# Two value phases of an expert layer: TensorE sums 512 columns of each row in place of 1024, VectorE 1536 in place of 1024

## The chip, the cores and the metric

The kernel runs on one core of a Trainium2 chip. The metric is the time of one execution on the device, in microseconds (us), lower is better. The engines have their own queues of instructions and meet only through semaphores: TensorE (PE in the rows: matrix products, with PEld for its weight loads), VectorE (DVE), ScalarE (ACT), GpSimd (POOL) and SyncE (SP). POOL and SP also start the transfers, which 16 DMA engines carry out.

## The reference

Two decoder layers are run over 256 prompt tokens and 32 sample tokens, each with 2048 features: a state-space mixer in layer 0, a gated recurrence in layer 1, and after each of them a mixer of experts. Each token picks 8 x 16 = 128 experts out of 16384. The part that matters here:

```python
def peer_ffn(h, w_q, sub_keys, u_emb, v_emb):
    idx, g = peer_retrieve(hf, w_q, sub_keys)        # top-16 of keys, top-16 of pairs, softmax
    ...
        u = u_emb[ib].astype(jnp.float32)
        act = jnp.einsum("nd,nhkd->nhk", xb.astype(jnp.float32), u)
        wgt = jax.nn.gelu(act, approximate=False) * gb
        v = v_emb[ib].astype(jnp.float32)
        return jnp.einsum("nhk,nhkd->nd", wgt, v)
```

So for each token 128 rows of the table u are fetched for dot products (a dot phase), and then 128 rows of the table v, which are weighted and summed (a value phase).

## The kernel before

Tokens lie on partitions: tiles 0 and 1 hold the 256 prompt tokens, tile 2 the 32 sample tokens four times over, so that it needs only 32 fetches per phase. One fetch, called a row below, is one gather of POOL (line 496): for each of 128 tokens the 2048 floats of its n-th expert, 1 MiB in all. It lands in one of 8 slots of a ring (`RING = 8`). All rows of all phases pass through this ring in order. POOL reuses a slot when VectorE is done with the row in it (`row_used`) and, in a value phase, TensorE too (`row_pe`); then it issues the next gather, for a row 8 further on.

A phase is named by layer and tile. Value phases come in the order of `PHASES`: (0, 0), (0, 2), (0, 1), (1, 0), (1, 2), (1, 1), with dot phases between them. In a value phase the sum of the weighted rows stays in PSUM in the four banks 4 to 7 (`high_banks`, 2048 columns). VectorE adds weight times row to the first columns (`v_row`, one SCALAR_TENSOR_TENSOR at line 1645 for each row). TensorE does the last columns: ScalarE scales the identity by the row's weights (`diagonals`, line 1259), and TensorE multiplies that diagonal matrix with the row, one matmul for each bank of 512 columns (line 923). A matmul of 32-bit floats stands as two records in the trace, so two banks are four records of a row. At the end VectorE adds TensorE's columns to the token tile (`last_columns`).

Other work is woven into the phases by row numbers (`Turns`: a step with number r is run after row r). Beside (0, 1) and (1, 0) run the queries and the choice of experts of the next layer or tile:

- TensorE multiplies the tokens with 16 slabs of weights (line 821), the first after row 16 of the phase and each next one 3 rows on, the last after row 61. A slab is 1 MiB that SP loads into a ring of 4 (`WRING`) when the product that used the slot is done. Behind every four products it makes key scores (lines 865 and 867).
- VectorE chooses the experts from the scores: top-16 lists of the keys, top-16 lists of the sums, and the expert numbers. Such a choice has three parts, and two rows stand between one part and the next. With the rows of the dot phase ahead taken off, `CHOOSE_ROW` puts the choices of (0, 1) after rows 30, 42, 54, 66 and 74, those of (1, 0) after rows 36, 48, 60 and 72. A softmax comes after row 84, and two norms come early in (0, 1).

Every row of VectorE waits for its gather and for VectorE's row before it:

```python
dve.wait_ge(row_in[r], 16 * (R + 1))
if n > 0:
    dve.wait_ge(row_used[(n - 1) % RING], ROUNDS * layer + V_AT[t] + (n - 1) // RING + 1)
```

Of the kernel before, what the change touches and what calls it, by code (L numbers as in the profile page):

```python
# [15 lines left out]
ALU = mybir.AluOpType  # L16
# [4 lines left out]
D = 2048  # L21
# [8 lines left out]
BANK = 512  # L30
# [22 lines left out]
PICKS_OF = [PICKS, PICKS, PICKS // COPIES]  # L53
# [7 lines left out]
LAST_HEAD_ISSUE = 6  # L61
LEAD = 3
GELU_SPLIT = 96
SHARE = 2
OWN = D - SHARE * BANK
DIAGS = 3
PHASES = [(0, 0), (0, 2), (0, 1), (1, 0), (1, 2), (1, 1)]

# [24 lines left out]
def values_before(layer, t):  # L93

    return sum(PICKS_OF[u] for _, u in PHASES[:PHASES.index((layer, t))])
# [59 lines left out]
def hybrid_step(nc, x, norms, slabs, keys, chan, s5_vec, s5_bc, s5_h0, lru_in, u0, v0, u1, v1,  # L155
                y_out, ys_out, s5p_out, s5s_out, lru_out):
    experts_u, experts_v = [u0, u1], [v0, v1]
    with ExitStack() as ctx:
        def sb(name, shape, dt=F32):
            return ctx.enter_context(nc.sbuf_tensor(name, shape, dt))  # L160

        def sem(name):
            return ctx.enter_context(nc.semaphore(name))


        X = sb("X", [P, TILES, D])
# [13 lines left out]
        ps = ctx.enter_context(nc.psum_tensor("ps", [P, 8, BANK], F32))  # L180
        hn_flat = HN[:].rearrange("p a b -> p (a b)")
        low_banks = ps[:, 0:4, :].rearrange("p b n -> p (b n)")
        high_banks = ps[:, 4:8, :].rearrange("p b n -> p (b n)")
        ht_flat = HT[:].rearrange("p a b -> p (a b)")

        def view(at, n, base=None):
            return (arena if base is None else base)[:, at:at + n]
# [58 lines left out]
        DG = [view(at - 512 + P * n, P) for n in range(DIAGS)]  # L246
# [23 lines left out]
        ring = view(0, RING * D).rearrange("p (r d) -> p r d", r=RING)  # L270
        ACC = HN[:, 2, :]
# [34 lines left out]
        row_used = [sem(f"row_used{r}") for r in range(RING)]  # L306
        row_pe = [sem(f"row_pe{r}") for r in range(RING)]
        diag_set, gate_set, v_done = sem("diag_set"), sem("gate_set"), sem("v_done")
# [314 lines left out]
        def _(pe):  # L623
# [289 lines left out]
            def value_rows(layer, t, turns):  # L913

                first = values_before(layer, t)
                if first > 0:
                    pe.wait_ge(v_done, PHASES.index((layer, t)))
                for n in range(PICKS_OF[t]):
                    R, r = ROUNDS * layer + V_AT[t] + n // RING, n % RING
                    pe.wait_ge(diag_set, first + n + 1)  # L920
                    pe.wait_ge(row_in[r], 16 * (R + 1))
                    for b in range(SHARE):
                        mm = nc.tensor.matmul(ps[:, 8 - SHARE + b, :], DG[(first + n) % DIAGS],  # L923
                                              ring[:, r, OWN + BANK * b:OWN + BANK * (b + 1)], start=(n == 0),
                                              stop=(n == PICKS_OF[t] - 1))
                    mm.then_inc(row_pe[r], 1)
                    turns.row()

            value_rows(0, 0, Turns(()))
            turns = Turns(sample_turn())  # L930
            value_rows(0, 2, turns)
            turns.finish()
            pe.wait_ge(norm_ht, 28)
            sample_sum(0)
            turned(7, 2)
            chain(0)
            turns = Turns(chain_queries(0))
            value_rows(0, 1, turns)
            turns.finish()
            turned(10, 1)  # L940
# [408 lines left out]
        def _(dve):  # L1349
            V = nc.vector  # L1350
# [151 lines left out]
            with dve.Fori(0, 4) as g:  # L1502
                for r in range(GROUP):
                    dve.wait_ge(bank_read, g * GROUP + (r + 3))
                    n = g * GROUP + r
# [126 lines left out]
            def v_row(layer, t, n):  # L1632

                R, r = ROUNDS * layer + V_AT[t] + n // RING, n % RING
                weight = WG[:, COL_AT[t] + n:COL_AT[t] + n + 1]
                dve.wait_ge(row_in[r], 16 * (R + 1))
                if n > 0:
                    dve.wait_ge(row_used[(n - 1) % RING], ROUNDS * layer + V_AT[t] + (n - 1) // RING + 1)
                row = ring[:, r, 0:OWN]
                if n == 0 and t == 2:  # L1640
                    V.tensor_scalar(high_banks[:, 0:OWN], row, weight, None, ALU.mult).then_inc(row_used[r], 1)
                    return
                total = X[:, t, 0:OWN] if n == 0 else high_banks[:, 0:OWN]
                to = high_banks[:, 0:OWN] if n < PICKS_OF[t] - 1 else ACC[:, 0:OWN] if t == 2 else X[:, t, 0:OWN]
                V.scalar_tensor_tensor(to, row, weight, total, ALU.mult, ALU.add).then_inc(row_used[r], 1)  # L1645

            def last_columns(layer, t):

                dve.wait_ge(row_pe[RING - 1], (values_before(layer, t) + PICKS_OF[t]) // RING + 1)
                if t == 2:  # L1650
                    V.tensor_copy(ACC[:, OWN:D], high_banks[:, OWN:D]).then_inc(v_done, 1)
                else:
                    V.tensor_tensor(X[:, t, OWN:D], high_banks[:, OWN:D], X[:, t, OWN:D], ALU.add).then_inc(v_done, 1)

            def u_rows(layer, t, turns, hn_count):

# [13 lines left out]
            def v_rows(layer, t, turns):  # L1670

                for n in range(PICKS_OF[t]):
                    if n == 0:
                        gate_weights(t, 0, GELU_SPLIT if t == 1 else PICKS_OF[t], 4 * layer + (1, 3, 2)[t])
                    if n == GELU_SPLIT and t == 1:
                        gate_weights(t, GELU_SPLIT, PICKS, 4 * layer + 4)
                    v_row(layer, t, n)
                    turns.row()
                last_columns(layer, t)
# [341 lines left out]
```

## Time and profile before

| | |
|---|---|
| median of 3 runs | 3864.35 us (3862.33 to 3864.55) |
| profiled execution, its own time and its span | 3864.24 us, 3862.4 us |
| PE busy (share of the span) | 2273.5 us (59%) |
| DVE busy | 2793.4 us (72%) |
| ACT busy | 679.6 us (18%) |
| POOL busy | 1472.3 us (38%) |
| DMA | 1404.76 MB, mean 364 GB/s |
| line 923, TensorE's columns of the rows | 1112.4 us in 2304 records |
| line 1645, VectorE's columns of the rows | 726.9 us in 564 instructions |

The busy times are sums over the whole span, in which engines work beside each other. The share of busy time is an average over stages with different limits; the value phase (0, 1) lies at 1900 to 2262 us of the span, (1, 0) at 2789 to 3139 us.

### The profile page before, as it was taken

The page shows a single profiled execution, that of the slowest core. Times are in us where ns is not written, and L with a number is a line of the kernel's source. Part 1 is how long each engine was busy: PE and PEld are TensorE (multiplying, and loading weights), DVE is VectorE, ACT ScalarE, POOL GpSimd, SP SyncE. Part 2 cuts the span into 40 slices and gives each one's busy share as a digit, 9 for nine tenths or more (in the row PEclk, how much of TensorE's full clock was granted, in tenths as well). Part 3 has the DMA queues.
Part 4 walks back from the last instruction along what each step waited for, and adds up shares of the span by engine and source line. Part 5 has one row for each costly group of instructions (what it writes and reads, how often), then busy time and mean ns, then how long its engine had stood idle before and what let it go on. Part 6 is the DMA issues. An engine that isn't in the chain of part 4 may idle for free.

```text
span 3862.4 us, 30909 instructions
## 1 busy us (share of the span) xinstructions
PE 2273.5 (59%) x9698; PEld 1381.5 (36%) x9698; DVE 2793.4 (72%) x3586; ACT 679.6 (18%) x1477; POOL 1472.3 (38%) x1739
## 2 busy tenths in 40 slices
PE   4667996000087788559599776470199773003776
PEld 2334775000022227549365246470055221001222
DVE  7996047999955558897757677868848658997554
ACT  6662121000011122120111112200011111000111
POOL 4885005434333343222323442223433434433432
PEclk8888998555599999779799998695599997556999
DMA  1002336999999999999999999999999999999998
GB/s 76 16 13 86 133 125 245 379 422 396 427 427 427 427 427 425 426 417 426 427 427 426 390 427 426 426 426 427 427 427 417 411 427 427 427 428 427 427 427 356
DMA packets 197426, 1404.76 MB, mean 364 GB/s; under 512 B 21952, under 2 KB 26304, under 8 KB 26768
## 3 DMA queue, kind: packets, MB, share of 16 engines
q0 software_dynamic: 167008, 1215.18, 74.9%
q1 hardware_dynamic: 30000, 187.74, 12.0%
q8 instruction: 73, 1.20, 0.1%
q14 instruction: 57, 0.47, 0.0%
q10 hardware_dynamic: 288, 0.18, 0.0%
HBM read 1399.77 MB, written 3.24 MB: 363 GB/s over the span
## 4 chain that ended last, share of the span: by engine, by line
DMA 38%; DVE 27%; PE 26%; issue 5%; ACT 4%; POOL 0%; POOLq 0%; DVEq 0%; ACTq 0%
DMA arena<-in_u_dram,ixs 26%; PE ps L923 16%; DVE arena L1629 12%; DMA arena<-in_v_dram,ixs 12%; PE ps L648 3%; ACT arena L1259 3%; PE ps L688 2%; DVE arena L1473 2%; PE ps L821 2%; DVE ps L1645 1%; DVE HN L1480 1%; DVE HN L1481 1%; DVE HN L1482 1%; DVE arena L1469 1%; DVE arena L1468 1%
## 5 line engine op out<-in xcount | busy, mean ns | idle before, releaser
L923 PE MATMUL ps<-arena 128*128 128x512 f32 x2304 | 1112.4, 612 | 1185.0 <-ACT arena L1259 1139.2
L1629 DVE CUSTOM_DVE_ANT_0 arena<-arena,ps 128x2048 f32<-128x2048 f32 x556 | 1257.4, 2286 | 193.4 <-DMA arena<-in_u_dram,ixs 175.0
L1645 DVE SCALAR_TENSOR_TENSOR ps<-arena,ps 128x1024 f32<-128x1024 f32 x564 | 726.9, 1289 | 588.1 <-DMA arena<-in_v_dram,ixs 576.0
L923 PEld LDWEIGHTS ps<-arena 128*128 128x128 f32 x2304 | 402.4, 191 | 1867.0 <-ACT arena L1259 938.6
L496 POOL DMA_INDIRECT arena<-in_u_dram,ixs x560 | 546.0, 975 | 1069.7 <-DVE arena L1629 1000.2
L496 POOL DMA_INDIRECT arena<-in_v_dram,ixs x576 | 556.3, 966 | 928.1 <-PE ps L923 719.5
L821 PE MATMUL ps<-HT,W 128*128 128x160 f32 (+1 forms) x3072 | 407.8, 295 | 70.6 <-ACT HN L1207 30.2
L821 PEld LDWEIGHTS ps<-HT,W 128*128 128x128 f32 x3072 | 402.4, 198 | 89.7 <-issue 74.5
L1259 ACT ACTIVATE arena<-ident,arena 128x128 f32<-128x128 f32 x576 | 228.2, 400 | 1003.0 <-PE ps L923 970.4
L849 PE MATMUL ps<-W,arena 128*128 128x128 f32 x1024 | 125.4, 283 | 41.0 <-DVE arena L1751 14.9
L849 PEld LDWEIGHTS ps<-W,arena 128*128 128x128 f32 x1024 | 121.7, 199 | 43.5 <-DVE arena L1751 15.1
L688 PE MATMUL ps<-HT,W 128*128 128x288 f32 x512 | 127.4, 410 | 0.0
L648 PE MATMUL ps<-arena,W 128*128 128x288 f32 x512 | 124.4, 406 | 0.7 <-ACT arena L1040 0.7
L833 PE MATMUL ps<-HN,W 128*128 128x160 f32 (+1 forms) x256 | 53.8, 381 | 98.6 <-ACT HN L1219 96.6
L1172 ACT ACTIVATE arena<-arena 128x32 f32<-128x32 f32 (+2 forms) x8 | 2.0, 260 | 623.6 <-DVE arena L1629 623.6
L688 PEld LDWEIGHTS ps<-HT,W 128*128 128x128 f32 x512 | 98.1, 193 | 27.8 <-issue 1.0
L648 PEld LDWEIGHTS ps<-arena,W 128*128 128x128 f32 x512 | 97.2, 190 | 27.5 <-issue 0.8
L754 PE MATMUL ps<-HN,arena 128*32 128x256 f32 x512 | 101.1, 481 | 0.0
L1506 DVE TENSOR_TENSOR arena<-arena 128x288 f32 x16 | 7.3, 458 | 127.2 <-ACT arena L1107 127.2
L1473 DVE TENSOR_TENSOR_SCAN arena<-arena 128x256 f32<-128x256 f32 x128 | 85.5, 736 | 0.5
L833 PEld LDWEIGHTS ps<-HN,W 128*128 128x128 f32 x256 | 48.9, 267 | 102.7 <-ACT HN L1219 98.9
L748 PE MATMUL ps<-HT,arena 128*128 128x256 f32 x32 | 18.8, 688 | 99.6 <-DVE HN L1482 99.6
(252 smaller groups left out, 2157.5 us busy)
## 6 DMA issues: line engine op xcount, KB each, us to landing
W<-in_slabs_dram SPq DMA_DIRECT2D x168, 1024.0 KB, 10.2
arena<-in_u_dram,ixs POOLq DMA_INDIRECT x576, 16.5
arena<-in_v_dram,ixs POOLq DMA_INDIRECT x576, 16.7
GB<-in_norms_dram POOLq DMA_DIRECT2D x4, 1024.0 KB, 6.2
arena<-in_s_bc_dram SPq DMA_DIRECT2D x32, 128.0 KB, 2.1
X<-in_x_dram SPq DMA_DIRECT2D x3, 1024.0 KB, 10.9
out_y_dram<-HN SPq DMA_DIRECT2D x2, 1024.0 KB, 6.3
arena<-in_keys_dram POOLq DMA_DIRECT2D x1, 1024.0 KB, 5.2
```

The source lines that it names most:

```text
L496: pool.indirect_dma_start(ring[:, r, :], None, table, bass.IndirectOffsetOnAxis(ap=ixs[:, side, r:r + 1], axis=0)).then_inc(row_in[r], 16)
L648: mm = nc.tensor.matmul(ps[:, r % 2, 0:NT], W[:, slot, P * k:P * (k + 1)], rhs[:, k, :], start=(k == 0), stop=(k == KT - 1))
L688: mm = nc.tensor.matmul(ps[:, r % 2, 0:NT], W[:, slot, P * k:P * (k + 1)], HT[:, k, :], start=(k == 0), stop=(k == KT - 1))
L754: mm = nc.tensor.matmul(ps[rows, 5, 0:SEQ], c, PR[n][:, q, :], start=False, stop=(n == 3), skip_group_check=True)
L821: mm = nc.tensor.matmul(ps[:, bank, 0:CHAIN_COLS[c]], W[:, slot, P * k:P * (k + 1)], HT1[c][:, k, :], start=(k == 0), stop=(k == KT - 1))
L833: mm = nc.tensor.matmul(ps[:, bank, 0:CHAIN_COLS[c]], W[:, slot, at:at + P], XC[c][g % 2][:, 2 * (b // 4) + e, :], start=(e == 0), stop=(e ...
L849: mm = nc.tensor.matmul(ps[:, bank, out], Y[:, k, :], W[:, slot, P * k:P * (k + 1)], start=(k == 0), stop=(k == KT - 1))
L923: mm = nc.tensor.matmul(ps[:, 8 - SHARE + b, :], DG[(first + n) % DIAGS], ring[:, r, OWN + BANK * b:OWN + BANK * (b + 1)], start=(n == 0), ...
L1259: A(DG[v % DIAGS], ident[:], ACT.Copy, scale=WG[:, col:col + 1]).then_inc(diag_set, 1)
L1473: ins = V.tensor_tensor_scan(dst[:, q, :], dec[:, k * QK + q:k * QK + q + 1].to_broadcast([P, SEQ]), src[:, q, :], 0.0, ALU.mult, ALU.add)
L1629: V.tensor_tensor_reduce(ring[:, r, :], ring[:, r, :], token, 1.0, 0.0, ALU.mult, ALU.add, AV[:, COL_AT[t] + n:COL_AT[t] + n + 1]).then_in ...
L1645: V.scalar_tensor_tensor(to, row, weight, total, ALU.mult, ALU.add).then_inc(row_used[r], 1)
```

## The change

The number of banks that TensorE sums is now a table by phase. In (0, 1) and (1, 0) it is one bank (512 columns), and VectorE sums 1536; the other four phases keep two banks and 1024 columns.

```diff
-SHARE = 2
-OWN = D - SHARE * BANK
+SHARE = {(0, 0): 2, (0, 2): 2, (0, 1): 1, (1, 0): 1, (1, 2): 2, (1, 1): 2}
+OWN = {phase: D - BANK * share for phase, share in SHARE.items()}
...
-                    for b in range(SHARE):
-                        mm = nc.tensor.matmul(ps[:, 8 - SHARE + b, :], DG[(first + n) % DIAGS],
-                                              ring[:, r, OWN + BANK * b:OWN + BANK * (b + 1)], start=(n == 0),
+                    share, own = SHARE[layer, t], OWN[layer, t]
+                    for b in range(share):
+                        mm = nc.tensor.matmul(ps[:, 8 - share + b, :], DG[(first + n) % DIAGS],
+                                              ring[:, r, own + BANK * b:own + BANK * (b + 1)], start=(n == 0),
                                               stop=(n == PICKS_OF[t] - 1))
...
-                row = ring[:, r, 0:OWN]
+                row = ring[:, r, 0:OWN[layer, t]]
...
-                total = X[:, t, 0:OWN] if n == 0 else high_banks[:, 0:OWN]
+                total = X[:, t, 0:OWN[layer, t]] if n == 0 else high_banks[:, 0:OWN[layer, t]]
...
-                    V.tensor_tensor(X[:, t, OWN:D], high_banks[:, OWN:D], X[:, t, OWN:D], ALU.add).then_inc(v_done, 1)
+                    V.tensor_tensor(X[:, t, OWN[layer, t]:D], high_banks[:, OWN[layer, t]:D], X[:, t, OWN[layer, t]:D], ALU.add).then_inc(v_done, 1)
```

TensorE's instructions in the value phase (0, 1), from its first row to the rows behind the first query product (L923 or L924 the rows, L800 the turning of the normed tokens, L821 the product of a slab), stand as follows before and after.

```order
L923 MATMUL ps<-arena 128x512 x12
L800 MATMUL ps<-ident,HN 128x128 x16
L923 MATMUL ps<-arena 128x512 x4
L800 MATMUL ps<-ident,HN 128x32 x16
L923 MATMUL ps<-arena 128x512 x8
L821 MATMUL ps<-HT,W 128x160 x16
L923 MATMUL ps<-arena 128x512 x6
```

```order
L924 MATMUL ps<-arena 128x512 x6
L800 MATMUL ps<-ident,HN 128x128 x16
L924 MATMUL ps<-arena 128x512 x2
L800 MATMUL ps<-ident,HN 128x32 x16
L924 MATMUL ps<-arena 128x512 x4
L821 MATMUL ps<-HT,W 128x160 x16
L924 MATMUL ps<-arena 128x512 x3
```

Every row has one matmul where it had two (the 6 rows ahead of the first turning have 6 for 12, the 3 rows behind the product 3 for 6), and all else stands after the same rows as before.

VectorE's instructions in the same phase, from the third part of the choice after row 66 to the first part of the one after row 74 (L1645 or L1646 the rows, L1555 to L1564, or one line on, the expert numbers, L1514 or L1515 the next top-16 lists), stand as follows before and after.

```order
L1645 SCALAR_TENSOR_TENSOR ps<-arena,ps 128x1024 x2
L1555 TENSOR_SCALAR arena<-arena 128x32
L1556 TENSOR_SCALAR arena<-arena 128x32
L1557 TENSOR_TENSOR arena<-arena 128x32
L1595 CAST arena<-arena 128x64
L1596 TENSOR_TENSOR arena<-arena,iota 128x1024
L1601 TENSOR_TENSOR arena<-arena 128x512 x2
L1560 TENSOR_REDUCE arena<-arena 128x64
L1564 SCALAR_TENSOR_TENSOR arena<-arena 128x32
L1645 SCALAR_TENSOR_TENSOR ps<-arena,ps 128x1024 x4
L1514 MAX arena<-ps 128x8 x4
```

```order
L1646 SCALAR_TENSOR_TENSOR ps<-arena,ps 128x1536 x2
L1556 TENSOR_SCALAR arena<-arena 128x32
L1557 TENSOR_SCALAR arena<-arena 128x32
L1558 TENSOR_TENSOR arena<-arena 128x32
L1596 CAST arena<-arena 128x64
L1597 TENSOR_TENSOR arena<-arena,iota 128x1024
L1602 TENSOR_TENSOR arena<-arena 128x512 x2
L1561 TENSOR_REDUCE arena<-arena 128x64
L1565 SCALAR_TENSOR_TENSOR arena<-arena 128x32
L1646 SCALAR_TENSOR_TENSOR ps<-arena,ps 128x1536 x4
L1515 MAX arena<-ps 128x8 x4
```

No instruction of VectorE has moved; the rows' instructions are longer.

## Rows read from the trace of the kernel before

**Rows 1.** The page, 40 equal slices of the span: bytes moved per second

```profile
GB/s 76 16 13 86 133 125 245 379 422 396 427 427 427 427 427 425 426 417 426 427 427 426 390 427 426 426 426 427 427 427 417 411 427 427 427 428 427 427 427 356
```

**Rows 2.** The page, the chain that ended last: share of the span by line

```profile
DMA arena<-in_u_dram,ixs 26%; PE ps L923 16%; DVE arena L1629 12%; DMA arena<-in_v_dram,ixs 12%; PE ps L648 3%; ACT arena L1259 3%; PE ps L688 2%; DVE arena L1473 2%; PE ps L821 2%; DVE ps L1645 1%; DVE HN L1480 1%; DVE HN L1481 1%; DVE HN L1482 1%; DVE arena L1469 1%; DVE arena L1468 1%
```

**Rows 3.** Windows: stretch, length, busy us of each engine, TensorE clock, DMA share, rate

```profile
1920.00:2100.00 180.00, 179.51 (x818) 120.18 (x817) 116.34 (x235) 26.68 (x77) 55.11 (x63) 1.00 1.01 426
...
2120.00:2160.00 40.00, 28.96 (x57) 10.24 (x56) 36.88 (x83) 7.32 (x17) 15.37 (x17) 0.96 0.89 337
2160.00:2260.00 100.00, 78.31 (x161) 27.25 (x162) 54.46 (x44) 15.14 (x38) 41.11 (x48) 1.00 1.01 427
2820.00:2980.00 160.00, 151.16 (x741) 97.06 (x740) 100.99 (x217) 23.09 (x67) 51.25 (x57) 1.00 1.01 426
2980.00:3040.00 60.00, 48.53 (x110) 18.40 (x109) 53.88 (x99) 11.62 (x27) 26.84 (x29) 1.00 0.97 387
```

**Rows 4.** Waits in (0, 1)'s value phase: who for whom, us, times, longest

```profile
POOL arena L496 <- PE ps L923: 169.3, 81, 8.1
...
POOL arena L496 <- DVE ps L1645: 45.3, 19, 5.9
```

**Rows 5.** The same view in (1, 0)'s value phase

```profile
POOL arena L496 <- PE ps L923: 121.1, 69, 4.3
...
POOL arena L496 <- DVE ps L1645: 67.8, 21, 6.0
```

**Rows 6.** Groups by line in (0, 1)'s value phase: busy, mean ns, idle before

```profile
L923 PE MATMUL ps<-arena 128*128 128x512 f32 x512 | 242.0, 612 | 81.7 <-ACT arena L1259 68.9 <-DMA arena<-in_v_dram,ixs 12.5 <-ACT HT L1185 0.4
L1645 DVE SCALAR_TENSOR_TENSOR ps<-arena,ps 128x1024 f32<-128x1024 f32 x126 | 162.4, 1289 | 111.7 <-DMA arena<-in_v_dram,ixs 105.6 <-DVE arena L1524 2.6
...
L1380 DVE SCALAR_TENSOR_TENSOR HN<-X,nrm,GB 128x2048 f32<-128x2048 f32 x2 | 4.7, 2352 | 0.1
```

**Rows 7.** VectorE's timeline, first choice of (0, 1): start, us, line, operation, count

```profile
1985.34 0.89 DVE L1514 MAX8 arena<-ps 128x8 f32<-128x128 f32 x4
...
1991.22 2.69 DVE L1645 SCALAR_TENSOR_TENSOR ps<-arena,ps 128x1024 f32<-128x1024 f32 x2 [0.32 <-DVE arena L1524]
1993.81 0.19 DVE L1548 CAST arena<-arena 128x64 f32<-128x64 uint32 x1
...
1999.47 2.69 DVE L1645 SCALAR_TENSOR_TENSOR ps<-arena,ps 128x1024 f32<-128x1024 f32 x2 [0.22 <-DVE arena L1524]
2002.07 0.18 DVE L1555 TENSOR_SCALAR arena<-arena 128x32 uint32<-128x32 uint32 x1
...
2006.69 5.46 DVE L1645 SCALAR_TENSOR_TENSOR ps<-arena,ps 128x1024 f32<-128x1024 f32 x4
```

**Rows 8.** TensorE's timeline in (0, 1)'s value phase

```profile
1940.00 4.51 PE L821 MATMUL ps<-HT,W 128*128 128x160 f32 x32
1944.34 5.31 PE L923 MATMUL ps<-arena 128*128 128x512 f32 x12
1949.49 4.51 PE L821 MATMUL ps<-HT,W 128*128 128x160 f32 x32
...
1981.00 4.51 PE L821 MATMUL ps<-HT,W 128*128 128x160 f32 x32
...
2094.41 17.69 PE L923 MATMUL ps<-arena 128*128 128x512 f32 x40
```

**Rows 9.** GpSimd's timeline, gathers issued: in brackets the wait and its releaser

```profile
1956.53 0.94 POOL L496 DMA_INDIRECT arena<-in_v_dram,ixs  x1 [5.07 <-PE ps L923]
...
2136.13 0.94 POOL L496 DMA_INDIRECT arena<-in_v_dram,ixs  x1 [5.34 <-DVE ps L1645]
```

**Rows 10.** DMA issues in (0, 1)'s value phase: count, KB, us to landing

```profile
W<-in_slabs_dram SPq DMA_DIRECT2D x16, 1024.0 KB, 9.2
arena<-in_v_dram,ixs POOLq DMA_INDIRECT x121, 15.7
```

**Rows 11.** A window of layer 1's dot phase, with TensorE half idle

```profile
2420.00:2460.00 40.00, 21.89 (x153) 21.55 (x154) 35.42 (x44) 11.38 (x30) 10.83 (x12) 0.71 1.01 426
```

More of the change, by code:

```diff
@@ L1638, in v_row @@
                     dve.wait_ge(row_used[(n - 1) % RING], ROUNDS * layer + V_AT[t] + (n - 1) // RING + 1)
-                row = ring[:, r, 0:OWN]
+                row = ring[:, r, 0:OWN[layer, t]]
                 if n == 0 and t == 2:
-                    V.tensor_scalar(high_banks[:, 0:OWN], row, weight, None, ALU.mult).then_inc(row_used[r], 1)
+                    V.tensor_scalar(high_banks[:, 0:OWN[layer, t]], row, weight, None, ALU.mult).then_inc(row_used[r], 1)
                     return
-                total = X[:, t, 0:OWN] if n == 0 else high_banks[:, 0:OWN]
-                to = high_banks[:, 0:OWN] if n < PICKS_OF[t] - 1 else ACC[:, 0:OWN] if t == 2 else X[:, t, 0:OWN]
+                total = X[:, t, 0:OWN[layer, t]] if n == 0 else high_banks[:, 0:OWN[layer, t]]
+                to = high_banks[:, 0:OWN[layer, t]] if n < PICKS_OF[t] - 1 else ACC[:, 0:OWN[layer, t]] if t == 2 else X[:, t, 0:OWN[layer, t]]
                 V.scalar_tensor_tensor(to, row, weight, total, ALU.mult, ALU.add).then_inc(row_used[r], 1)
@@ L1650, in last_columns @@
                 if t == 2:
-                    V.tensor_copy(ACC[:, OWN:D], high_banks[:, OWN:D]).then_inc(v_done, 1)
+                    V.tensor_copy(ACC[:, OWN[layer, t]:D], high_banks[:, OWN[layer, t]:D]).then_inc(v_done, 1)
                 else:
-                    V.tensor_tensor(X[:, t, OWN:D], high_banks[:, OWN:D], X[:, t, OWN:D], ALU.add).then_inc(v_done, 1)
+                    V.tensor_tensor(X[:, t, OWN[layer, t]:D], high_banks[:, OWN[layer, t]:D], X[:, t, OWN[layer, t]:D], ALU.add).then_inc(v_done, 1)
             def u_rows(layer, t, turns, hn_count):
```

## The prediction

> **What bounds the kernel now.** The page's rate of transfer comes first: from a quarter of the span on it stands at 426 or 427 GB/s in nearly all slices [rows 1]. That is a flat top, so most of the span costs what its bytes cost, whatever the engines do beside it. At 427 GB/s one row or slab of 1 MiB (1.0486 MB) takes 2.456 us.
>
> The chain of waits tells another story: the rows' matmuls of line 923 hold 16% of it, VectorE's rows of line 1645 only 1% [rows 2]. So the two phases are looked at by windows [rows 3]. From 1920 to 2100 us TensorE is busy 179.51 of 180 us, and yet the DMA engines move 426 GB/s. TensorE and DMA are both full there, and taking work from TensorE can't make bytes arrive sooner. Only two stretches fall short: 2120 to 2160 us at 337 GB/s, and 2980 to 3040 us at 387. The idle time in them is 40 x (1 - 337/427) = 8.4 us in (0, 1) and 60 x (1 - 387/427) = 5.6 us in (1, 0), 14.0 us together. In the first of these VectorE is busy 36.88 of 40 us and TensorE 28.96, and GpSimd, which issues the gathers, waits there 5.34 us at a time for VectorE's rows [rows 9]. Over both phases GpSimd waits longer for TensorE, 169.3 and 121.1 us, than for VectorE, 45.3 and 67.8 [rows 4, 5]; but the long waits for TensorE are the even 5.07 us of the product stretch [rows 9], under which the rate stays full. So the choices on VectorE, not the matmuls, empty the queue of gathers.
>
> **What the change removes.** Half of the 512 records of line 923 in each phase, 612 ns each [rows 6]: 256 x 0.612 = 157 us of issue and overlap in name, about 0.86 us for each row, since three rows with two banks take 5.15 us between products (1949.49 - 1944.34, [rows 8]). All of it lies under full transfers: 0 us on the path, and a gain only where TensorE's slots delay gathers into an idle queue. `last_columns` shrinks by 512 columns once per phase, under the gathers of the next phase: 0. No transfer, semaphore or queue entry of SyncE or GpSimd is moved.
>
> **What it adds.** 128 instructions of VectorE in each phase grow from 1024 to 1536 columns. The trace has no such shape on this line. From 1289 ns at 1024 to 2352 ns at 2048 columns (line 1380, operands in SBUF, [rows 6]) halfway is 1820 ns, +0.53 us. Scaling 1289 with the columns gives 1934, +0.64 us, as the upper end. Zero is excluded, since the same operation grows between those two rows. I take +0.53 us. Between back-to-back rows the pitch is now (5.46 - 1.29) / 3 = 1.39 us [rows 7], so 1.92 us after.
>
> That is below 2.456 us, so where VectorE only sums rows it is free. It matters around the choices, which I work out as a lag of VectorE behind the arriving rows. A choice costs, without its rows, 1991.22 - 1985.34 = 5.88, 1999.47 - 1993.81 = 5.66 and 2006.69 - 2002.07 = 4.62, together 16.2 us [rows 7], and four rows belong to it. Among products, three rows come with one slab, in 4 x 2.456 = 9.82 us, a row every 3.27; behind the last slab a row comes every 2.456.
>
> - Lag from one choice now: 16.2 + 4 x 1.39 less 4 x 3.27 = 8.7 us among products, 16.2 + 5.6 - 9.8 = 11.9 us behind them. Each further row wins back 1.88 or 1.07 us.
> - After: 16.2 + 4 x 1.92 = 23.9, so 10.8 us among products and 14.1 us behind them. Each row wins back 1.35 or only 0.54 us.
>
> The ring gives VectorE a lead before the queue of gathers runs dry; what the lag has above the lead is lost. **(0, 1) now:** the choices after rows 66 and 74 lie behind the last product, with four rows between them: 11.9 - 4 x 1.07 + 11.9 = 19.5; with 8.4 us measured idle, the lead is 11.1 us. **After:** the choice after row 54 leaves 10.8 - 6 x 1.35 - 2 x 0.54 = 1.6; then 1.6 + 14.1 - 4 x 0.54 + 14.1 = 27.6, less 11.1: 16.5 us idle, **+8.1**. The three choices ahead of them lag 10.8, inside the lead.
>
> **(1, 0) now:** choices after rows 60 and 72, eight rows between: 11.9 - 8.6 + 11.9 = 15.2; with 5.6 measured, the lead is 9.6. **After:** 14.1 - 8 x 0.54 + 14.1 = 23.9, less 9.6: 14.3, **+8.7**. The two earlier choices lag 10.8, up to 1.2 us each above the lead. I take these as 0, because in that stretch it is TensorE that holds the slots (the 5.07 us waits), and it lets go 0.86 us a row sooner. Nothing later can win the lost time back, since the dot phases that follow run at full rate too [rows 1].
>
> Sum: 8.1 + 8.7 = +16.8 us on the profiled execution's own 3864.24 us, which is the median of the runs within 0.2 us: **3881 us**.
>
> Bounds. At the upper price (pitch 2.03) the lag is 14.5 and 11.2, the gain per row 0.43 and 1.24; the same sums give about +11 and +13 (with the early choices spilling), 3888 us. A lead of 8 us instead gives +18 and +15, 3897 us. A lead of 15.7 us, the time from issue to landing that a gather has now [rows 10], gives 27.6 - 15.7 - 8.4 = +3.5 and 23.9 - 15.7 - 5.6 = +2.6, 3870 us. The measured idle times speak for 9.6 to 11.1.
>
> **Rivals.**
>
> 1. *TensorE paces, and the change makes it faster.* A cycle of four products, their scores and 12 rows takes 41.0 us (1940.00 to 1981.00), against 39.3 us for its 16 MiB, and behind the last product TensorE works through 10 rows without a pause in 17.69 us [rows 8]. If the matmuls set the pace, the change gives back 4 x 1.7 = 7 us, so 3857 us, at most 3864 - 7 - 14 = 3843. Against it: 426 GB/s through that stretch, so the missing time isn't in the DMA engines. It also needs VectorE's longer lag to fit: the lead would have to exceed 27.6 - 8.4 = 19.2 us, where 8 slots are 8 x 2.456 = 19.6 us in all. Chance 0.05.
>
> 2. *The lead grows and hides it.* TensorE gives slots back sooner, also when it would have been behind at row 64, so the lead goes up toward 15.7 us: +6 us, 3870 us; the bound of "no change" is at a lead near 14.9. For it: TensorE's 10 rows behind. Against: in (1, 0), where TensorE has pauses (151.16 of 160 us), the lead came out no longer. Chance 0.14.
>
> 3. *TensorE's clock falls.* With one matmul a row and a wait for the next gather, the granted clock may leave 1.00 [rows 3]. At 2.4 GHz three rows and a product then take 2.6 + 4.34 = 6.9 us of the 9.82; at 1.2 GHz they would take 13.9 us, 4 us more than the bytes, 16 x 4 = 64 us for each phase that stays there throughout. It decides at a mean clock of 6.9 / 9.82 = 0.70. The nearest row has 21.89 of 40 us busy at a granted clock of 0.71 and 426 GB/s [rows 11], so the engine would have to fall deeper than there. The same chance covers a shorter lead at the early choices; a quarter of the price in one phase, or a lead of 8 us, ends near 3898 us. The Trainium skill's page "TensorE: Matmul & The Clock Gate", section "HAM oscillation — how this bites in real kernels", says that a kernel whose matmuls wait for transfers between bursts drops to the half clock again and again. By that rule this rival would be the rule here and not the exception; the trace has granted clocks between 0.71 and 1.00 in such mixed stretches, so it agrees in part. Chance 0.17.
>
> **How the numbers follow.** My forecast has 0.64, with 3874 to 3892 us as its own range. The ends take in rival 2 (3870) and most of rival 3: 3869 to 3897. A measurement of this kernel tells about 0.2% (7.7 us) from no change. Faster by that much: nearly all of rival 1, 0.04. Within it: rival 2's 3870 and the rest, 0.14. Slower: 0.82.
>
> **What would show it.** In the trace after: line 1646 at 1.82 us for 1536 columns; about half of line 924's records in the two phases; idle time of the DMA near 16 us behind row 66 of (0, 1) and near 14 us behind row 60 of (1, 0), with GpSimd waiting there for VectorE; its waits for TensorE much smaller; full rate in the product stretch. I am wrong if the rate stays at 427 GB/s behind the last product (lead longer than 15 us), if it sags among the products with VectorE never idle (lead shorter), or if it sags there with TensorE full at a clock under 0.7.

## The result, and the profile after

The changed kernel takes 3883.88 us (median of 5 runs, 3882.75 to 3884.58); the kernel before took 3862.33 us beside it (median of 5, 3861.49 to 3864.55). The ratio is 1.0054, 95% interval [1.0039, 1.0068]: 0.54% or about 21 us slower. The forecast was 3881 us, 17 us slower.

Of the page after, the rate in 40 slices and the chain that ended last by line, which answer to [rows 1] and [rows 2]:

```profile
GB/s 75 16 13 86 140 120 251 383 417 407 427 427 427 427 427 425 426 415 426 427 426 403 374 426 426 427 426 427 427 426 391 381 427 427 427 428 427 427 427 359
...
DMA arena<-in_u_dram,ixs 26%; DMA arena<-in_v_dram,ixs 13%; PE ps L924 13%; DVE arena L1630 13%; DVE ps L1646 5%; PE ps L648 3%; PE ps L688 2%; ACT arena L1260 2%; DVE arena L1474 2%; DVE arena L1525 1%; DVE arena L1518 1%; DVE arena L1519 1%; DVE HN L1481 1%; DVE arena L1522 1%; DVE HN L1482 1%
```

The top at 427 GB/s is where it was. The slices that had sagged sag further: 390 GB/s in (0, 1) is now 403 and 374, and 417 and 411 in (1, 0) are 391 and 381. In the chain line 924 has lost three points and VectorE's rows, now line 1646, have gone from 1% to 5%; a chain of waits follows who came last, so it names VectorE only where it really was last.

The windows of the same stretches as in [rows 3], with the sagging ones cut where they sag after (columns as there):

```profile
1920.00:2100.00 180.00, 149.47 (x710) 101.82 (x708) 146.90 (x235) 27.75 (x79) 58.03 (x65) 0.94 1.01 427
2100.00:2180.00 80.00, 47.57 (x54) 12.18 (x54) 74.52 (x147) 11.73 (x28) 25.80 (x30) 0.61 0.85 333
2180.00:2260.00 80.00, 57.88 (x66) 14.29 (x64) 62.71 (x37) 13.03 (x33) 34.01 (x39) 0.63 1.01 428
2820.00:2960.00 140.00, 104.64 (x544) 73.57 (x544) 104.46 (x159) 22.20 (x62) 44.31 (x49) 0.90 1.01 427
2960.00:3060.00 100.00, 68.00 (x173) 27.95 (x174) 93.43 (x160) 15.52 (x39) 34.61 (x38) 0.66 0.89 347
```

Among the products the rate is full, as before. The idle time of the DMA engines is 80 x (1 - 333/427) = 17.6 us in (0, 1), where it was 8.4, and 100 x (1 - 347/427) = 18.7 us in (1, 0), where it was 5.6: 36.3 us in place of 14.0, or 22 us more, which is the 21 us of the result within what two rates of three digits can tell. In both stretches VectorE is busy 93% of the time. TensorE's granted clock has fallen to 0.61 to 0.66 in the row stretches (between the levels of 1.2 and 2.4 GHz), and to 0.90 and 0.94 among the products.

Who held the gathers, first in (0, 1) and then in (1, 0), answering to [rows 4] and [rows 5]:

```profile
POOL arena L496 <- DVE ps L1646: 155.8, 68, 6.7
...
POOL arena L496 <- PE ps L924: 64.5, 34, 7.7
```

```profile
POOL arena L496 <- DVE ps L1646: 149.7, 75, 6.7
...
POOL arena L496 <- PE ps L924: 61.9, 34, 5.6
```

The two have changed places: GpSimd now waits 155.8 and 149.7 us for VectorE and 64.5 and 61.9 for TensorE. Most of these waits fall under a full rate and cost nothing; those in the sagging stretch do, of which two rows of its timeline stand here, answering to the second of [rows 9]:

```profile
2111.11 0.95 POOL L496 DMA_INDIRECT arena<-in_v_dram,ixs  x1 [6.65 <-DVE ps L1646]
...
2141.97 0.95 POOL L496 DMA_INDIRECT arena<-in_v_dram,ixs  x1 [6.57 <-DVE ps L1646]
```

In each of these waits of over 6 us VectorE is busy with the first part of a choice and then with the first row behind it (the part begins at 2102.51 and at 2133.46 us). The groups by line in (0, 1), answering to [rows 6]:

```profile
L1646 DVE SCALAR_TENSOR_TENSOR ps<-arena,ps 128x1536 f32<-128x1536 f32 x126 | 229.5, 1822 | 53.4 <-DMA arena<-in_v_dram,ixs 45.0 <-DVE arena L1525 2.6
L924 PE MATMUL ps<-arena 128*128 128x512 f32 x256 | 192.9, 857 | 135.0 <-DMA arena<-in_v_dram,ixs 73.8 <-ACT arena L1260 60.8 <-ACT HT L1186 0.4
```

VectorE's row costs 1822 ns, against 1820 estimated; TensorE's records have halved to 256 and grown from 612 to 857 ns each with the lower clock.

### The profile page after: what moved, and what is told of

Read it like the earlier page. It is cut to its first block, busy times and chain, and to the rows that moved or that the text cites. A ratio compares the mean times of both kernels' runs of the same rounds, so it can differ in the third digit from the quotient of the medians.

```text
span 3882.3 us, 29885 instructions
## 1 busy us (share of the span) xinstructions
PE 2180.1 (56%) x9186; PEld 1307.8 (34%) x9186; DVE 2927.8 (75%) x3586; ACT 679.6 (18%) x1477; POOL 1479.9 (38%) x1739
## 4 chain that ended last, share of the span: by engine, by line
DMA 39%; DVE 31%; PE 21%; issue 5%; ACT 3%; POOL 0%; POOLq 0%; DVEq 0%; ACTq 0%
DMA arena<-in_u_dram,ixs 26%; DMA arena<-in_v_dram,ixs 13%; PE ps L924 13%; DVE arena L1630 13%; DVE ps L1646 5%; PE ps L648 3%; PE ps L688 2%; ACT arena L1260 2%; DVE arena L1474 2%; DVE arena L1525 1%; DVE arena L1518 1%; DVE arena L1519 1%; DVE HN L1481 1%; DVE arena L1522 1%; DVE HN L1482 1%
## 5 line engine op out<-in xcount | busy, mean ns | idle before, releaser
L924 PE MATMUL ps<-arena 128*128 128x512 f32 x1792 | 1016.6, 686 | 1288.4 <-ACT arena L1260 1108.7
L1646 DVE SCALAR_TENSOR_TENSOR ps<-arena,ps 128x1024 f32<-128x1024 f32 (+1 forms) x564 | 861.2, 1527 | 475.8 <-DMA arena<-in_v_dram,ixs 459.4
L924 PEld LDWEIGHTS ps<-arena 128*128 128x128 f32 x1792 | 324.3, 207 | 1944.4 <-ACT arena L1260 984.4
L821 PE MATMUL ps<-HT,W 128*128 128x160 f32 (+1 forms) x3072 | 413.2, 297 | 78.3 <-ACT arena L1210 34.4
L821 PEld LDWEIGHTS ps<-HT,W 128*128 128x128 f32 x3072 | 408.8, 200 | 103.6 <-issue 87.2
## 6 DMA issues: line engine op xcount, KB each, us to landing
arena<-in_u_dram,ixs POOLq DMA_INDIRECT x576, 16.5
```

The lines of the kernel that those rows point to most:

```text
L821: mm = nc.tensor.matmul(ps[:, bank, 0:CHAIN_COLS[c]], W[:, slot, P * k:P * (k + 1)], HT1[c][:, k, :], start=(k == 0), stop=(k == KT - 1))
L924: mm = nc.tensor.matmul(ps[:, 8 - share + b, :], DG[(first + n) % DIAGS], ring[:, r, own + BANK * b:own + BANK * (b + 1)], start=(n == 0), ...
```

## The experiments

Eight kernels in two batches, each timed beside the kernel before on the same chip. The edits up to that of half the addition are made to the changed kernel. The kernel before measured 3862.87 us there in the first batch (22 runs) and 3862.88 us in the second (27 runs). The windows under the runs are always those of 2100 to 2180 us and 2960 to 3060 us, if not said otherwise. The kernel before has in them

```profile
2100.00:2180.00 80.00, 61.67 (x128) 22.55 (x126) 67.64 (x151) 13.61 (x33) 32.64 (x36) 0.98 0.95 381
...
2960.00:3060.00 100.00, 84.00 (x235) 36.59 (x234) 80.08 (x161) 18.37 (x45) 41.28 (x46) 1.00 0.98 402
```

which is 8.6 and 5.9 us idle, within 0.3 us of the 8.4 and 5.6 of the narrower windows in [rows 3].

**The change in (0, 1) alone, and in (1, 0) alone.**

```diff
-SHARE = {(0, 0): 2, (0, 2): 2, (0, 1): 1, (1, 0): 1, (1, 2): 2, (1, 1): 2}
+SHARE = {(0, 0): 2, (0, 2): 2, (0, 1): 1, (1, 0): 2, (1, 2): 2, (1, 1): 2}
```

> Change in (0, 1) alone; (1, 0) keeps two banks. If VectorE's lag at the crowded choices costs the time, the two phases add up: about +9 us on the kernel before (its own idle time in the changed kernel's trace is 17.6 us against 8.4), and the window behind row 66 of (0, 1) falls to about 330 GB/s while (1, 0) keeps its 5.6 us. If TensorE's lower clock carries over from one phase to the next, the two parts do not add up to +21.

```diff
-SHARE = {(0, 0): 2, (0, 2): 2, (0, 1): 1, (1, 0): 1, (1, 2): 2, (1, 1): 2}
+SHARE = {(0, 0): 2, (0, 2): 2, (0, 1): 2, (1, 0): 1, (1, 2): 2, (1, 1): 2}
```

> Change in (1, 0) alone. By VectorE's lag: about +12 us on the kernel before (18.7 us idle in the changed kernel's trace against 5.6), with (0, 1) at its old 8.4 us. The sum of this and the run with (0, 1) alone should be +21 us within 4.

Measured: 3871.37 us for (0, 1) alone, ratio 1.0021 [1.0012, 1.0030], +8.5 us; 3875.86 us for (1, 0) alone, ratio 1.0032 [1.0020, 1.0044], +13.0 us. The windows of the first and then of the second run:

```profile
2100.00:2180.00 80.00, 45.39 (x53) 11.80 (x51) 74.53 (x147) 11.72 (x28) 26.00 (x29) 0.62 0.85 332
...
2960.00:3060.00 100.00, 85.51 (x264) 39.65 (x263) 82.36 (x165) 18.14 (x45) 40.75 (x45) 1.00 0.98 401
```

```profile
2100.00:2180.00 80.00, 60.49 (x124) 21.95 (x123) 67.57 (x151) 13.33 (x32) 32.05 (x36) 0.98 0.95 378
...
2960.00:3060.00 100.00, 67.14 (x147) 24.16 (x145) 93.28 (x158) 16.73 (x42) 36.13 (x41) 0.68 0.89 351
```

Each phase sags alone where its own rows are long, and the other keeps the rate that it had. 8.5 + 13.0 = 21.5 us, the whole within a microsecond, so nothing that these times can show is carried from one phase to the next.

**TensorE's half of the change without VectorE's.** VectorE keeps 1024 columns; 512 columns of the rows are left out of the sum.

```diff
+SUMS = {phase: D - 2 * BANK for phase in SHARE}
...
-                row = ring[:, r, 0:OWN[layer, t]]
+                row = ring[:, r, 0:SUMS[layer, t]]
```

(and so for `total` and `to` of `v_row`).

> TensorE sums one bank as in the change, but VectorE keeps its 1024 columns in both phases; columns 1024 to 1535 of the rows are left out of the sum. By VectorE's lag nothing is lost: the time of the kernel before within 4 us, or up to 7 us less if TensorE's shorter hold of the slots lengthens the lead. If TensorE's fall to the half clock in the row stretches is what costs, this run shows the whole +21 us.

Measured: 3863.37 us, ratio 1.0000 [0.9991, 1.0009]. Its windows, with the product stretches (1920 to 2100 and 2820 to 2960 us) too:

```profile
1920.00:2100.00 180.00, 149.65 (x690) 103.38 (x690) 116.20 (x237) 26.12 (x74) 56.40 (x64) 0.91 1.01 427
2100.00:2180.00 80.00, 53.76 (x60) 13.67 (x60) 67.36 (x151) 12.21 (x30) 30.54 (x33) 0.63 0.95 379
2820.00:2960.00 140.00, 110.02 (x571) 78.92 (x572) 84.90 (x162) 19.55 (x57) 44.49 (x50) 0.88 1.01 426
2960.00:3060.00 100.00, 74.65 (x144) 24.02 (x142) 80.42 (x161) 17.97 (x44) 40.90 (x46) 0.68 0.99 406
```

TensorE's clock falls as in the changed kernel, to 0.63 and 0.68 in the row stretches and 0.91 and 0.88 among the products, and it costs nothing. The shorter hold of the slots gains nothing either: the idle time is 80 x (1 - 379/427) = 9.0 and 100 x (1 - 406/427) = 4.9 us, the 8.4 and 5.6 of before within a microsecond.

**VectorE's half without TensorE's.** VectorE sums 1536 columns, and TensorE still does two matmuls a row, both into its last bank, whose 512 columns take in 512 columns too many.

```diff
-                    for b in range(share):
-                        mm = nc.tensor.matmul(ps[:, 8 - share + b, :], DG[(first + n) % DIAGS],
-                                              ring[:, r, own + BANK * b:own + BANK * (b + 1)], start=(n == 0),
-                                              stop=(n == PICKS_OF[t] - 1))
+                    for b in range(2):
+                        bank, col = (7, D - 2 * BANK + BANK * b) if share == 1 else (6 + b, own + BANK * b)
+                        mm = nc.tensor.matmul(ps[:, bank, :], DG[(first + n) % DIAGS],
+                                              ring[:, r, col:col + BANK],
+                                              start=(n == 0 and (share == 2 or b == 0)),
+                                              stop=(n == PICKS_OF[t] - 1 and (share == 2 or b == 1)))
```

> VectorE sums 1536 columns as in the change, but TensorE still does two matmuls a row, both into its last bank, so its last 512 columns take in 512 columns too many. By VectorE's lag: +21 us or somewhat more, up to +30, since TensorE holds slots as long as before and takes away lead. If TensorE's clock costs, the time is that of the kernel before, since TensorE is as busy as there.

Measured: 3883.54 us, ratio 1.0053 [1.0040, 1.0067]. The same four windows:

```profile
1920.00:2100.00 180.00, 179.51 (x817) 120.06 (x816) 146.78 (x235) 26.51 (x76) 53.44 (x62) 1.00 1.01 423
2100.00:2180.00 80.00, 59.33 (x117) 22.55 (x116) 74.52 (x147) 12.96 (x32) 27.90 (x31) 0.89 0.87 339
2820.00:2960.00 140.00, 130.89 (x634) 82.81 (x633) 104.59 (x158) 21.97 (x61) 44.24 (x49) 1.00 1.01 427
2960.00:3060.00 100.00, 80.68 (x244) 38.37 (x242) 93.50 (x160) 15.80 (x40) 34.85 (x38) 0.93 0.90 349
```

The whole loss is there (16.5 and 18.3 us idle, and 1.7 us more among the products at 423 GB/s), with TensorE at clock 1.00 among the products and 0.89 to 0.93 in the row stretches. Together the last two runs are the change taken apart: VectorE's half +20.7 us, TensorE's half +0.5 us.

**Half of VectorE's addition.** TensorE as in the change, VectorE 1280 columns; 256 columns are left out of the sum.

```diff
+SUMS = {phase: D - 2 * BANK + (256 if share == 1 else 0) for phase, share in SHARE.items()}
...
-                row = ring[:, r, 0:OWN[layer, t]]
+                row = ring[:, r, 0:SUMS[layer, t]]
```

> TensorE sums one bank as in the change, VectorE 1280 columns in the two phases, half of what the change adds; 256 columns of the rows are left out of the sum. By the lag behind the crowded choices: pitch 1.66 us, a lag of 13.0 behind the last product and 0.80 us won back per row, so +3.3 us in (0, 1) and +4.4 in (1, 0), with what is left over from the choices among products +8 to +11 us in all. If VectorE only turned into the limit at 1536 columns as a whole, this run stays within 3 us of the kernel before.

Measured: 3871.88 us, ratio 1.0023 [1.0014, 1.0033], +9.0 us, inside the 8 to 11 us of the lag.

```profile
2100.00:2180.00 80.00, 49.88 (x57) 12.58 (x56) 72.68 (x150) 12.53 (x30) 28.73 (x32) 0.63 0.91 360
...
2960.00:3060.00 100.00, 72.98 (x169) 27.05 (x168) 89.55 (x160) 17.53 (x44) 40.12 (x45) 0.69 0.94 381
```

80 x (1 - 360/427) = 12.6 and 100 x (1 - 381/427) = 10.8 us idle. A row of 1.56 us (1555 ns in its trace) is far below the 2.456 us in which the next one arrives, and yet it costs: the loss stands in the stretches of the crowded choices, and among the products the rate is 426 and 427 GB/s.

**The choices further apart, in the kernel before and in the changed kernel.** The same edit in both:

```diff
-CHOOSE_ROW = [[158, 170, 182, 194, 202], [196, 208, 220, 232]]
-SOFT_ROW = [212, 244]
+CHOOSE_ROW = [[158, 170, 182, 198, 214], [196, 208, 224, 240]]
+SOFT_ROW = [224, 252]
```

> The kernel before (two banks, 1024 columns) with its late choices further apart: after rows 70 and 86 of (0, 1) in place of 66 and 74, after rows 64 and 80 of (1, 0) in place of 60 and 72, the softmax 12 and 8 rows later. By the lag: 12 rows of 1.07 us win back the 11.9 us of a choice, so each of the four choices loses only what is above the lead, 0.8 and 2.3 us, 6 us in place of 14: 8 us faster, 3855 us. If the idle time is not owed to the crowding of the choices, no change.

> The changed kernel (one bank, 1536 columns) with the same rows for its choices as the run of the kernel before with choices apart. By the lag: 12 rows win back only 6.4 us, so 14.1 - 6.4 + 14.1 less the lead, about 11 and 14 us idle in place of 17.6 and 18.7: 9 to 12 us below the changed kernel, 3873 us, and still some 18 us above the kernel before with choices apart. If VectorE's choices do not matter, 3884 us.

Measured: the kernel before with choices apart 3858.84 us, ratio 0.9990 [0.9981, 0.9999], 4 us faster where 8 were expected; the changed kernel with choices apart 3874.53 us, ratio 1.0030 [1.0018, 1.0043] to the kernel before, 9.4 us below the changed kernel's 3883.88 us, as expected, and 15.7 us above the kernel before with choices apart, where some 18 were expected. Windows, of the kernel before with choices apart, then of the changed one (there with 2180 to 2260 us, into which the sagging now reaches):

```profile
2100.00:2180.00 80.00, 62.86 (x131) 22.17 (x130) 65.83 (x149) 13.55 (x32) 30.84 (x35) 1.00 1.00 413
...
2960.00:3060.00 100.00, 83.52 (x233) 36.02 (x231) 79.71 (x161) 18.21 (x45) 41.47 (x46) 1.00 0.99 404
```

```profile
2100.00:2180.00 80.00, 55.74 (x62) 14.05 (x60) 73.34 (x143) 12.64 (x30) 25.78 (x31) 0.59 0.93 382
2180.00:2260.00 80.00, 50.95 (x63) 13.65 (x62) 68.51 (x43) 12.63 (x32) 35.25 (x41) 0.65 0.99 407
...
2960.00:3060.00 100.00, 64.65 (x151) 24.78 (x149) 93.39 (x154) 17.41 (x44) 36.08 (x41) 0.70 0.93 369
```

Moving the choices alone, with every instruction as long as it was, takes back nearly half of the loss of the change: idle are 8.43 + 3.75 = 12.2 us in (0, 1) and 13.6 us in (1, 0), where about 11 and 14 were expected. In the kernel before it takes 8.4 us idle to 80 x (1 - 413/427) + 80 x (1 - 424/427) = 3.2 us in (0, 1), the second of these from its window of 2180 to 2260 us at 424 GB/s, but hardly moves the 5.6 us in (1, 0), which are 100 x (1 - 404/427) = 5.4 now. By the lag there was little to win there: each of the two choices by itself stands 2.3 us above the lead of 9.6, so 4.6 us were to remain, and in (0, 1), with its longer lead of 11.1, 1.6 us. In all 8.6 us are idle where 6 were expected.

**The parts of a choice apart.** The kernel before (two banks), with four rows and not two between the parts of each choice, so that none of them outgrows the lead.

```diff
-CHOOSE_ROW = [[158, 170, 182, 194, 202], [196, 208, 220, 232]]
-SOFT_ROW = [212, 244]
+CHOOSE_ROW = [[158, 170, 182, 194, 210], [196, 208, 220, 236]]
+SOFT_ROW = [224, 252]
...
-                yield row + 2
+                yield row + 4
...
-                yield row + 4
+                yield row + 8
```

> The kernel before (two banks, 1024 columns) with the three parts of each choice 4 rows from each other in place of 2, and the last choice after row 82 of (0, 1) and row 76 of (1, 0). By the lag: a part costs at most 5.9 us and four rows win back 4.3, so the lag of a choice peaks near 7.6 us, below the lead of 9.6: the idle time of 14 us goes nearly away, 3849 to 3851 us, faster than both kernels. If the lead is shorter than 7 us, it gains less than the run with choices apart.

Measured: 3857.85 us, ratio 0.9987 [0.9978, 0.9996], 5 us faster than the kernel before and 26 us faster than the changed one: faster than both, but not by the 12 us expected.

```profile
2100.00:2180.00 80.00, 63.60 (x133) 22.46 (x132) 70.32 (x155) 14.68 (x36) 32.32 (x38) 1.00 1.01 426
...
2960.00:3060.00 100.00, 83.93 (x218) 34.69 (x218) 80.71 (x162) 18.78 (x46) 40.95 (x46) 1.00 1.01 422
```

Both stretches are all but full, as expected: 0.2 and 1.2 us idle. But two short dips stand in its trace where the kernel before had none, at 2480 to 2510 us and 3220 to 3240 us, in the dot phase behind (0, 1) and at the end of (1, 2), some 2 us each. What brings them there was not tried, and they do not make up the whole of what is missing.

## Why the prediction was right, point by point

- *The bytes bound the stretch, not TensorE.* Right. TensorE's half of the change gained 0 us, though line 923 held 16% of the chain of waits and TensorE was busy 179.51 of 180 us [rows 2, 3].
- *The price of a longer row, +0.53 us.* Right: 1822 ns measured against 1820.
- *The lag behind a choice, against the lead of the ring.* Right as a mechanism: the loss lies where it was put, is there with VectorE's half alone, is about half as large with half the dose, and shrinks when the choices move apart. The lead itself was fitted to the idle time of the kernel before and not measured; no run varied the ring.
- *(0, 1): 16.5 us idle.* 17.6 in the trace, and +8.5 us in the run of that phase alone against +8.1.
- *(1, 0): 14.3 us idle.* Mis-sized: 18.7 in the trace and +13.0 us alone against +8.7. The step is the one that took the two earlier choices of (1, 0) as 0. It rested on a row every 3.27 us among products, with 1.35 us won back a row, so that a choice was forgotten before the next, and on the 1.2 us that their lag stands above the lead costing nothing. VectorE's timeline there shows otherwise. In the changed kernel, from the choice after row 48 to that after row 60 (which begins at 2977.68 us):

```profile
2934.53 1.82 DVE L1646 SCALAR_TENSOR_TENSOR ps<-arena,ps 128x1536 f32<-128x1536 f32 x1 [0.86 <-DMA arena<-in_v_dram,ixs]
2937.29 1.82 DVE L1646 SCALAR_TENSOR_TENSOR ps<-arena,ps 128x1536 f32<-128x1536 f32 x1 [0.94 <-DMA arena<-in_v_dram,ixs]
...
2944.90 3.76 DVE L1646 SCALAR_TENSOR_TENSOR ps<-arena,ps 128x1536 f32<-128x1536 f32 x2 [0.32 <-DVE arena L1525]
...
2954.24 3.76 DVE L1646 SCALAR_TENSOR_TENSOR ps<-arena,ps 128x1536 f32<-128x1536 f32 x2 [0.22 <-DVE arena L1525]
...
2962.47 15.29 DVE L1646 SCALAR_TENSOR_TENSOR ps<-arena,ps 128x1536 f32<-128x1536 f32 x8
```

After the third part eight rows run without a gap, 15.29 us, right up to the next choice, so VectorE came to row 60 late. In the kernel before, the rows in the same place:

```profile
2951.70 5.46 DVE L1645 SCALAR_TENSOR_TENSOR ps<-arena,ps 128x1024 f32<-128x1024 f32 x4
2957.76 1.29 DVE L1645 SCALAR_TENSOR_TENSOR ps<-arena,ps 128x1024 f32<-128x1024 f32 x1 [0.60 <-DMA arena<-in_v_dram,ixs]
2960.19 1.29 DVE L1645 SCALAR_TENSOR_TENSOR ps<-arena,ps 128x1024 f32<-128x1024 f32 x1 [1.14 <-DMA arena<-in_v_dram,ixs]
```

There the lag is worked off after four rows, and from then on a row arrives every 2.44 us and not every 3.27. SyncE's queue shows why. Of the slabs, (0, 1) loads 16 in the changed kernel and (1, 0) only 12; the last load of (1, 0) is issued at 2947.33 us, and its last product begins at 2976.65:

```profile
W<-in_slabs_dram SPq DMA_DIRECT2D x16, 1024.0 KB, 8.8
```

```profile
W<-in_slabs_dram SPq DMA_DIRECT2D x12, 1024.0 KB, 8.9
...
2947.33 0.33 SPq L362 DMA_DIRECT2D W<-in_slabs_dram  x1
...
2976.65 3.73 PE L821 MATMUL ps<-HT,W 128*128 128x128 f32 x32
```

The ring `WRING` lets the loads run four products ahead. In (0, 1) SyncE goes on with the slabs of later products, and its last load there, at 2081.05 us, comes as the last product ends; in (1, 0) nothing more is to be loaded, so the stretch with "a row every 2.456" begins about twelve rows before the last product, ahead of row 60 and not behind row 61. So a row of 1.92 us wins back about 0.5 us there, not 1.35. Two windows ahead of row 60 show the other part of the miss:

```profile
2960.00:2970.00 10.00, 8.89 (x42) 6.46 (x43) 9.62 (x8) 1.37 (x4) 3.41 (x4) 0.83 0.98 401
2970.00:2980.00 10.00, 9.59 (x70) 7.83 (x68) 9.44 (x19) 1.37 (x4) 4.96 (x6) 1.00 1.00 415
```

They hold 10 x (1 - 401/427) + 10 x (1 - 415/427) = 0.9 us idle, behind waits of GpSimd of up to 6.52 us for VectorE in the choice after row 48, where 0 was taken. With the lead of 9.6 us as it was, the other 17.8 us mean that some 3.5 us were left over at row 60 (17.8 - 14.3); a lag of 9.6 less eight times 0.54 would leave 5.3, so the way is right and the size is not exact. By the same reckoning 17.6 - 16.5 + 1.6 = 2.7 us were left at row 66 of (0, 1), where 1.6 were taken. The end of the loads is read from the trace; no run varied it.
- *A bound.* For a lead of 8 us the sum of (1, 0), 15.9 - 5.6 + 2 x 2.8, is +15.9 and not +15; the upper end would have been 3898 us.
- *Rival 1, TensorE paces.* Fallen, by the run with TensorE's half alone.
- *Rival 2, the lead grows.* Fallen: idle time is the same whether TensorE holds a slot for one bank or two, in the short and the long form of VectorE's rows.
- *Rival 3, the clock falls.* It fell, in the row stretches even below the 0.70 that would matter among the products (0.61 to 0.66), but there it stayed at 0.90 and 0.94, and it cost nothing: the run with TensorE's half alone has nearly the same clocks and the time of before. The Trainium skill's page "TensorE: Matmul & The Clock Gate", section "HAM oscillation — how this bites in real kernels", describes a kernel whose short bursts of matmuls lose the full clock again and again in the waits for transfers between them. The trace agrees in that; but the waits of the page's case are longer than its bursts, while here a burst of 2.05 us stands behind a wait of 0.41 us (the first row of the last section). The page also reckons a loss of time from the half clock; none shows here, 3863.37 us against 3862.87, since the matmuls had idle time to grow into.

## What to carry to other kernels

Where the transfers run at a flat top, an engine that is busy all the time and holds much of the chain of waits may still be worth nothing to relieve; look for the stretches in which the rate sags and at who is last there. An engine that is below its share on the average (1.92 us a row against 2.456) can still starve the queue when its other work comes in lumps: reckon its lag over the lumps against the lead that the ring gives, and spread the lumps before moving work. Count the competing loads of each stretch in the queue that issues them, and not by the products that use them: a ring of four slabs ends its loads four products early. Moving work onto the engine with the lumps costs twice, through the longer lump and through the slower recovery.

## What the hardware showed that was not expected

That the clock might fall was foreseen as rival 3; how little the row would then save was not. TensorE's granted clock in the row stretches went from between 0.98 and 1.00 down to between 0.61 and 0.66 when one of two matmuls per row was taken away, and the remaining matmul then took about as long as the two had: a row's two records 2.05 us at the low level, against 1.96 us for a row's four at the full one. TensorE's timeline in the row stretch of (0, 1), a row of the changed kernel (granted clock 0.50, that is 1.2 GHz, from 2235 to 2240 us) and one of the kernel before (1.00, that is 2.4 GHz, from 2110 to 2115 us):

```profile
2235.57 2.05 PE L924 MATMUL ps<-arena 128*128 128x512 f32 x2 [0.41 <-DMA arena<-in_v_dram,ixs]
```

```profile
2112.60 1.96 PE L923 MATMUL ps<-arena 128*128 128x512 f32 x4 [0.50 <-ACT arena L1259]
```

TensorE's busy time over (0, 1) therefore fell only from 242.0 to 192.9 us where half of the records were gone.
